# A mixture of experts on one core: experts in an order ranked by their tokens, four of them in rounds of 128 columns

## The reference

```python
g_idx = argmax(x @ router_g + b_g)                      # 1 of 4 groups
e_sel = (x @ router_e + b_e)[g_idx]                     # 8 logits in the group
top_v, top_i = top_k(e_sel, 2)
w = softmax(top_v) * softmax(g_logits)[g_idx]
out += w * (silu(x @ w1[e]) * (x @ w3[e])) @ w2[e]      # for both experts e
```

```
13 14 23 10 28 28 11 21 | 35  8 40 40 43 27 29 20 | 76 47 37 45 42 74 100 29 | 20 17 20 23 36 24 36 24
```

## Time and profile before

| | before |
|---|---|
| runs, us | 788.22, 794.74, 794.53; median 794.53 |
| profiled execution, us | 788.86 |
| its span, us | 787.1 |
| mean granted TensorE clock | 0.926 |
| PE / DVE / ACT / POOL busy | 84% / 38% / 26% / 10% |
| DMA | 189.86 MB, mean 241 GB/s |

### The profile page before, as it was taken

One profiled execution on the slowest core, in us unless ns is written; L12 is line 12 of the kernel. 1 busy time (PEld: TensorE's weight loads), 2 busy tenths in 40 slices (PEclk: granted clock), 3 DMA queues, 4 the chain that ended last, 5 costly groups with the idle time before them and its releaser, 6 DMA issues.

```text
span 787.1 us, 11931 instructions
## 1 busy us (share of the span) xinstructions
PE 660.6 (84%) x4993; PEld 470.0 (60%) x4993; DVE 300.1 (38%) x605; ACT 208.4 (26%) x359; POOL 80.8 (10%) x93
## 2 busy tenths in 40 slices
PE   4999997998999989999899549988878788889730
PEld 3999995678999989957787433333323233333210
DVE  3645575348533455785131821211111111111128
ACT  4613223044543334451031411211111111111113
POOL 0000002300002201000021111121111111111100
PEclk8899999999999999999899859999999889999965
DMA  9741312122755334899901955999999999979544
GB/s 284 227 132 55 108 54 80 33 73 68 201 134 195 108 101 132 286 300 307 381 22 68 409 191 226 420 419 420 421 419 420 420 420 420 414 287 417 244 167 165
DMA packets 76653, 189.86 MB, mean 241 GB/s; under 512 B 9878, under 2 KB 56658, under 8 KB 61736
## 3 DMA queue, kind: packets, MB, share of 16 engines
q1 hardware_dynamic: 63020, 145.09, 49.9%
q10 hardware_dynamic: 7404, 31.26, 9.7%
q0 software_dynamic: 6176, 12.76, 4.4%
HBM read 184.30 MB, written 16.66 MB: 255 GB/s over the span
## 4 chain that ended last, share of the span: by engine, by line
PE 59%; DMA 26%; DVE 7%; issue 3%; ACT 2%; SPq 1%; ACTq 1%; POOL 0%; POOLq 0%; DVEq 0%
DMA w<-exp_w 21%; PE ps L1844 11%; PE ps L1480 11%; PE ps L1482 11%; PE ps L1481 11%; PE ps L1586 4%; PE ps L1476 3%; PE ps L1871 2%; PE ps L1667 2%; DMA raw<-cache_mem_k 2%; DMA xe<-x_rows,gids 1%; DMA xs_rows<-x_sample 1%; PE ps L1604 1%; PE ps L1729 1%; DVE rstd L918 1%
## 5 line engine op out<-in xcount | busy, mean ns | idle before, releaser
L1844 PE MATMUL ps<-w,xeT 128*64 128x512 f32 x576 | 147.0, 669 | 31.2 <-DMA w<-exp_w 29.9
L1480 PE MATMUL ps<-xH,w_h 128*128 128x260 f32 x512 | 149.6, 292 | 11.7 <-DVE xL L944 5.2
L1482 PE MATMUL ps<-xL,w_h 128*128 128x260 f32 x512 | 146.5, 286 | 0.0
L1481 PE MATMUL ps<-xH,w_l 128*128 128x260 f32 x512 | 146.5, 286 | 0.0
L1844 PEld LDWEIGHTS ps<-w,xeT 128*64 128x64 f32 x576 | 50.8, 152 | 126.1 <-issue 121.5
L1480 PEld LDWEIGHTS ps<-xH,w_h 128*128 128x128 f32 x512 | 98.6, 193 | 17.2 <-DVE w_l L905 7.7
L1481 PEld LDWEIGHTS ps<-xH,w_l 128*128 128x128 f32 x512 | 98.4, 192 | 0.2
L1482 PEld LDWEIGHTS ps<-xL,w_h 128*128 128x128 f32 x512 | 98.4, 192 | 0.0
L905 DVE TENSOR_TENSOR w_l<-raw,w_h 128x2048 fp32r<-128x2048 f32 x28 | 64.1, 2289 | 35.3 <-ACT w_h L599 35.2
L1871 PE MATMUL ps<-w,aT 128*64 128x512 f32 x288 | 67.5, 611 | 11.1 <-DVE aT L1395 11.1
L1388 DVE SCALAR_TENSOR_TENSOR gated<-ps,rs_slot,silu 128x256 f32<-128x256 f32 x16 | 7.7, 484 | 158.3 <-ACT silu L841 158.3
(11 more groups left out here) (297 smaller groups left out, 884.6 us busy)
## 6 DMA issues: line engine op xcount, KB each, us to landing
w<-exp_w SPq DMA_DIRECT2D x81, 1024.0 KB, 19.1
w<-exp_w ACTq DMA_DIRECT2D x27, 1024.0 KB, 11.1
raw<-w_in SPq DMA_DIRECT2D x8, 1024.0 KB, 6.6
raw<-cache_mem_k SPq DMA_DIRECT2D x8, 1024.0 KB, 6.7
raw<-cache_mem_v SPq DMA_DIRECT2D x8, 1024.0 KB, 12.2
raw<-xa_wk SPq DMA_DIRECT2D x4, 1024.0 KB, 5.8
raw<-xa_wv SPq DMA_DIRECT2D x4, 1024.0 KB, 5.7
raw<-xa_wq SPq DMA_DIRECT2D x4, 1024.0 KB, 5.1
```

What stands on the lines that cost most here:

```text
L1480: pe.matmul(out, h1, h2, start=start, stop=False)
L1481: pe.matmul(out, l1, h2, start=False, stop=False)
L1482: return pe.matmul(out, h1, l2, start=False, stop=stop)
L1844: last = pe.matmul(mm[0][half, j, :], xeT[j][:, k, half], w13[s][:, :, k, :], start=k == 0, stop=k == KT_D - 1)
```

## The change

- Routing: PE counts the tokens of each expert twice, as a row on all partitions and as a column of 32 partitions (`count_ready`). DVE makes a key from count and number, compares all with all (`less`, `more_than`), and PE sums `less` to a rank. Experts 0 to 3, loaded already, get keys below all others. The four largest of the others get places 4, 9, 14 and 19 (`HEAVY`), the rest follow in falling order. Tables by place (`order`) and by rank (`blocks`) come out of one-hot matmuls, and the start of each expert's further items from a triangular matmul in place of five shifted additions on DVE.
- Rounds: places 4, 9, 14 and 19 are a round each, of 128 columns (`cap`), the others go in pairs: 16 rounds (still `PAIRS`) hold 28 places. Places 28 to 31 are the first four items of the loop, and items of over-full experts follow from the second pass on. `loops` is 1 when there are none.
- Loads: SP reads the expert's number from `order` in registers (`expert_at`) and issues all three matrices, w2 after a wait on `y_done`; ACT issues none. Expert 4's load became that of place 4 and waits for `order_ready`; `row_hot` lies elsewhere.
- `who`, `e_all` and the products are made by single operations for both choices and all tiles. `r2` sums `sumsq` and the last square, `zt[1]`, on PE, so that POOL adds seven blocks. POOL makes the constant rows by iota ahead, and PE turns two of them (`con`) between `so` and the second half of `wo`.

```diff
 CAP = P // 2
-PAIRS = EXPERTS // 2
-MORE_ITEMS = 2 * T // CAP
+SINGLES = 4
+ROUNDS = [(0, 1), (2, 3)]
+for _ in range(SINGLES):
+    p = ROUNDS[-1][-1] + 1
+    ROUNDS += [(p,), (p + 1, p + 2), (p + 3, p + 4)]
+ROUNDS += [(p, p + 1) for p in range(24, 28, 2)]
+PAIRS = len(ROUNDS)
+FIXED = 28
+OVER = 2 * T // CAP
+MORE_ITEMS = EXPERTS - FIXED + OVER
 COLS = PAIRS + MORE_ITEMS // 2 + 2
-KEY = 2048
 RING = 5
+ALL_ROUNDS = ROUNDS + [(28, 29), (30, 31)]
+BLOCK = [2 * q + n for q, r in enumerate(ALL_ROUNDS) for n in range(len(r))]
+HEAVY = [r[0] for r in ROUNDS if len(r) == 1]
+BY_RANK = HEAVY + [p for p in range(4, EXPERTS) if p not in HEAVY] + list(range(4))
+OVER_BLOCK = 2 * len(ALL_ROUNDS)
...
+            + ["ss", "sp", "or00", "or01", "or10", "or11", "so", "con", "r2", "lg", "pos", "list"])
...
-        row_hot = at("row_hot", [P, 2, NT, P], F32, e_at[4])
+        row_hot = at("row_hot", [P, 2, NT, P], F32, v_at)
...
-            sp.wait_ge(tv_ready, len(TV_ORDER))
-            load_gate_up(4, 4)
-            load_down(4, 4)
-            for q in range(2, PAIRS):
-                for e in (2 * q, 2 * q + 1):
-                    if e >= RING:
-                        sp.wait_ge(hid_ready, (e - RING) // 2 + 1)
-                        load_gate_up(e % RING, e)
+            sp.wait_ge(order_ready, 1)
+
+            def expert_at(p):
+
+                return sp.value_load(order[0:1, bass.ds(p, 1)], min_val=0, max_val=EXPERTS - 1)
+
+            e = expert_at(4)
+            load_gate_up(4, e)
+            load_down(4, e)
+            for q, places in enumerate(ROUNDS):
+                coming = [p + RING for p in places if p + RING < FIXED]
+                if coming:
+                    which = [expert_at(p) for p in coming]
+                    sp.wait_ge(hid_ready, q + 1)
+                    for p, e in zip(coming, which):
+                        load_gate_up(p % RING, e)
+                    sp.wait_ge(y_done, q + 1)
+                    for p, e in zip(coming, which):
+                        load_down(p % RING, e)
...
+                for r, slots in enumerate(((3, 4), (0, 1))):
+                    which = [expert_at(it * 4 + (FIXED + 2 * r + n)) for n in range(2)]
...
-                for e in (2 * q + RING, 2 * q + RING + 1):
-                    if e < EXPERTS:
-                        act.dma_start(w2s[e % RING][:].rearrange("p k d -> p (k d)"), w2[e]).then_inc(w2_in[e % RING], 16)
...
+            src = take("con")
+            dve.tensor_copy(con[:], src[0:EXPERTS, 0:2]).then_inc(tv_used, 1)
+            dve.tensor_tensor(through_of[:], upper[0:EXPERTS, 0:EXPERTS], ident[0:EXPERTS, 0:EXPERTS], ALU.add)
...
-            for j in range(NT):
-                last = dve.tensor_tensor(e_all[:, j], e_log[:, j], sel4[:, j], ALU.mult)
-            link(last)
+            link(dve.tensor_tensor(e_all[:], e_log, sel4, ALU.mult))
...
+                one = e_one[:, i].rearrange("p t (o e) -> p t o e", o=1).broadcast_to([P, NT, NG, NE])
+                link(dve.tensor_tensor(who[:, i].rearrange("p t (g e) -> p t g e", g=NG), one, sel4, ALU.mult))
+            dve.tensor_tensor(both[:], who[:, 0], who[:, 1], ALU.add).then_inc(who_ready, 1)
...
+            dve.wait_ge(route_made, 4)
+            dve.wait_ge(count_ready, 1)
+            counts = mm[0][:, 0, 0:EXPERTS]
+            dve.tensor_copy(count_p[:], mm[0][0:EXPERTS, 0, EXPERTS:EXPERTS + 1])
+            dve.scalar_tensor_tensor(key_p[:], mm[0][0:EXPERTS, 0, EXPERTS:EXPERTS + 1], float(EXPERTS), con[:, 0:1], ALU.mult, ALU.add)
+            link(dve.scalar_tensor_tensor(key_f[:], counts[0:EXPERTS], float(EXPERTS), key_row[0:EXPERTS], ALU.mult, ALU.add))
+            dve.tensor_scalar(less[:], key_f[:], key_p[:, 0:1], None, ALU.is_lt).then_inc(less_ready, 1)
+            link(dve.tensor_scalar(more_than[:], key_f[:], key_p[:, 0:1], None, ALU.is_gt))
+            link(dve.tensor_reduce(rank_p[:], more_than[:], AX_X, ALU.add))
+            link(dve.tensor_scalar(caps_p[:], rank_p[:], float(SINGLES), 1.0, ALU.is_lt, ALU.add))
+            dve.wait_ge(rank_ready, 1)
+            ranks = mm[0][:, 1, 0:EXPERTS]
+            dve.tensor_scalar(at_rank[:], ranks[0:EXPERTS], part_no[0:EXPERTS, 0:1], None, ALU.is_equal).then_inc(at_rank_ready, 1)
+            dve.tensor_scalar(caps[:], ranks, float(SINGLES), 1.0, ALU.is_lt, ALU.add)
+            link(dve.scalar_tensor_tensor(rank_f[:], caps_p[:], -float(CAP), count_p[:], ALU.mult, ALU.add))
+            link(dve.tensor_scalar(over_i[:, 0:1], rank_f[:], float(CAP - 1), 0.0, ALU.add, ALU.max))
+            link(dve.tensor_scalar(over_i[:, 1:2], over_i[:, 0:1], 6, None, ALU.arith_shift_right))
+            dve.tensor_copy(over_f[:], over_i[:, 1:2]).then_inc(over_ready, 1)
+            dve.tensor_scalar(at_place[:], rank_row[0:EXPERTS], rank_p[:, 0:1], None, ALU.is_equal).then_inc(at_place_ready, 1)
+
...
+            src = take("pos")[:, 0:NT * EXPERTS].rearrange("p (t e) -> p t e", t=NT)
+            dve.scalar_tensor_tensor(ptmp[:], each(caps[:]).broadcast_to([P, NT, EXPERTS]), -float(CAP), src,
+                                     ALU.mult, ALU.add).then_inc(tv_used, 1)
...
+            over_two = ptmp[:].rearrange("p (o t) e -> p o t e", o=1).broadcast_to([P, 2, NT, EXPERTS])
+            link(dve.tensor_tensor(wtmp[:], who[:], over_two, ALU.mult))
+            dve.tensor_reduce(place[:, 0], wtmp[:], AX_X, ALU.add)
+            dve.wait_ge(block_ready, 1)
+            link(dve.tensor_tensor(blocks[:], mm[1][:, 0, 0:EXPERTS], caps[:], ALU.add))
+            link(dve.tensor_scalar(blocks[:], blocks[:], 1.0 - CAP, float(CAP * OVER_BLOCK), ALU.mult, ALU.add))
+            dve.wait_ge(starts_ready, 1)
+            link(dve.scalar_tensor_tensor(packed[:], mm[1][:, 1, 0:EXPERTS], float(CAP), blocks[:], ALU.mult, ALU.add))
+            packed_b = each(packed[:]).broadcast_to([P, 2 * NT, EXPERTS])
+            flat = "p i t e -> p (i t) e"
+            link(dve.tensor_tensor(wtmp[:].rearrange(flat), who[:].rearrange(flat), packed_b, ALU.mult))
+            link(dve.tensor_reduce(place[:, 1], wtmp[:], AX_X, ALU.add))
+            link(dve.tensor_copy(place_i[:], place[:, 1]))
...
+            dve.tensor_scalar(bits[:, 0], place_i[:], CAP - 1, None, ALU.bitwise_and)
+            link(dve.tensor_scalar(bits[:, 1], place_i[:], 6, None, ALU.arith_shift_right))
+            link(dve.scalar_tensor_tensor(bits[:, 2], place[:, 0], 0.0, bits[:, 1], ALU.is_ge, ALU.mult))
+            link(dve.tensor_tensor(bits[:, 3], bits[:, 2], bits[:, 0], ALU.add))
+            link(dve.scalar_tensor_tensor(bits[:, 4], bits[:, 3], float(CAP), place[:, 0], ALU.mult, ALU.add))
+            dve.tensor_scalar(slot_i[:, 0], bits[:, 4], P - 1, None, ALU.bitwise_and)
+            link(dve.tensor_scalar(slot_i[:, 1], bits[:, 4], 7, None, ALU.arith_shift_right))
+            link(dve.tensor_copy(slot_f[:], slot_i[:]))
...
+            dve.wait_ge(place_ready, 1)
+            dve.tensor_copy(order[0:1, 0:EXPERTS], mm[0][0:1, 1, EXPERTS:2 * EXPERTS]).then_inc(order_ready, 1)
+            link(dve.tensor_copy(through[:], mm[1][:, 1, EXPERTS:2 * EXPERTS]))
...
-            dve.tensor_scalar(more_of[0:1], ends_n[0:1], float(EXPERTS - 1), None, ALU.min)
+            dve.tensor_scalar(order[0:1, EXPERTS:EXPERTS + OVER], ends_n[0:1], float(EXPERTS - 1), None, ALU.min)
...
+            link(dve.tensor_scalar(loops[0:1], total, 0.0, 1.0, ALU.is_gt, ALU.add))
+            for i in range(1, OVER // 4):
...
+            pe.wait_ge(route_made, 2)
+            out = open_tv("con")
+            pe.matmul(out[0:EXPERTS, 0:1], key_row[0:1, :], ones[0:1, 0:1], start=True, stop=True)
+            pe.matmul(out[0:EXPERTS, 1:2], block_row[0:1, :], ones[0:1, 0:1], start=True, stop=True).then_inc(tv_ready, 1)
...
-            pe.wait_ge(sq_added, 16)
             out = open_tv("r2")
+            pe.wait_ge(sq_added, 15)
+            pe.wait_ge(sq_ready, 16)
             for j, (t0, n) in enumerate(TILES):
-                last = pe.matmul(out[0:n, j:j + 1], sumsq[:, t0:t0 + n], ones[:, 0:1], start=True, stop=True)
+                for i, of in enumerate((sumsq, zt[1])):
+                    last = pe.matmul(out[0:n, j:j + 1], of[:, t0:t0 + n], ones[:, 0:1], start=i == 0, stop=i == 1)
...
+            pe.wait_ge(mm_used, len(MM_ORDER))
+            for j, (_, n) in enumerate(TILES):
+                pe.matmul(mm[0][:, 0, 0:EXPERTS], ones[0:n, :], both[0:n, j, :], start=j == 0, stop=j == NT - 1)
+            for j, (_, n) in enumerate(TILES):
+                last = pe.matmul(mm[0][0:EXPERTS, 0, EXPERTS:EXPERTS + 1], both[0:n, j, :], ones[0:n, 0:1],
+                                 start=j == 0, stop=j == NT - 1)
+            last.then_inc(count_ready, 1)
             out = open_tv("pos")
-            pe.matmul(out[:, 0:(NT + 1) * EXPERTS], upper[:], both[:].rearrange("p t e -> p (t e)"), start=True, stop=False)
...
```

(89 more changed lines are left out.)

92 lines of the change are left out of this document (54 added, 38 removed).

## The result

| | before | after |
|---|---|---|
| median of four runs, us | 794.57 (788.22 to 794.74) | 759.40 (756.11 to 761.22) |
| profiled execution / its span, us | 788.86 / 787.1 | 761.22 / 759.5 |
| mean granted TensorE clock | 0.926 | 0.937 |

The ratio is 0.9581, with a 95% interval of 0.9546 to 0.9617, which is 33 us less; the two medians of the table lie 35.2 us apart. The changed kernel was run again beside later experiments and gave 757.13 against 791.58, a ratio of 0.9568 (0.9542 to 0.9593).

The account below looks back on a forecast made before the run. The rounds were taken as bound by the DMA bytes of the weights. Terms -30.1 - 3 + 3.1 + 0.5 - 1.0 = -30.5 us gave 758.4 from the profiled execution and 764.1 from the median; forecast the middle, 761, range 751 to 774.

Parts of the forecast that it names:

- Bytes, 36 experts to 32, 30.1 us: Weight loads of the rounds: four experts fewer, 12.6 MB at 418 GB/s, 30.1 us saved.
- which limit holds: Rounds: DMA lets the last `hidden` begin near 702, PE at 689, so DMA stays the limit by some 13 us.
- Rounds of one expert cost as much as pairs: Rounds on PE: one expert takes 7.2 and 3.6 us against a pair's 7.04 and 3.65; period 12.7, bounds 12.7 to 13.1.
- PE at full clock to round 13, first wait at round 14: Rounds on PE: granted clock 1.00 without weight waits through round 13, then a first wait of 5 to 10 us.
- The hole at the loop, -3: DMA dip where the loop begins, 307 of 418 GB/s: larger backlog fills it, gain 0 to 5.8 us, taken as 3.
- Routing, +3.1: Routing chain on PE and DVE before the rounds: `slot_f` done 3.1 us later, bounds 2 and 6.
- First gather, -1.0: Start of the rounds: less of place 4's load left beside the gather, landing 1.0 us sooner.
- One queue, nothing: Weight loads all on SP's queue: waits for `y_done` make nothing late, issue lies beside `hidden`, cost nothing.
- A: Rival: weights fully continuous, routing free; 36.4 us saved, 752 against the profiled execution; chance 0.07 (below 752).
- C: Rival: gathers in the rounds land late, over 1% slower from landings of 20.2 us; 810 at 21 us; chance 0.04.
- D: Rival: token counts force a second loop pass, 36 experts loaded in 20 rounds; 789 to 798 us; chance 0.06.
- B: Rival: PE becomes the rounds' limit, period 13.5 us in place of 12.7; 765 to 773 us; chance 0.15.

## Why the prediction was right

The forecast was 761 us, with a range of 751 to 774, and the measured 759.4 lies in it. The mechanism is the one described: the bytes of four experts, saved in a stage bound by the DMA. That 759.4 lies as near as 1.6 us to 761 is in part luck. The sum of -30.5 gives 764.1 from the median of the runs, and the 761 is halfway from there to the 758.4 that it gives from one fast execution; the medians themselves moved by 33 to 35 us. Point by point:

- **Bytes, 36 experts to 32, 30.1 us.** Measured 96 loads, one pass, 92.6 MB in the stretch, and 30.4 to 30.5 us less from first to last `hidden`. The size is right. The reason given ahead of it, 12.6 MB at 418 GB/s, was not enough by itself: without loads in the loop the kernel before gains 4 us. What made the bytes count is that light rounds lie between heavy ones, so that DMA and PE both stay full. The prediction's part on which limit holds had this, but as a check and not as a condition.
- **Rounds of one expert cost as much as pairs.** 7.13 + 3.70 against 7.04 + 3.65; period 12.8 to 12.9. Inside the bounds. The page "TensorEngine Tiling (Array Packing)" of the Trainium skill, section "Theoretical Speedup", gives up to a factor of two at 64 or less, and the trace agrees: 32 instructions at 64 columns, for two experts, take what 16 at 128 take for one.
- **PE at full clock to round 13, first wait at round 14.** The first wait was 0.86 us at round 10, the first large one at round 13, one round early, with 3.5 us where 5 to 10 had been reckoned. The granted clock is 1.00 up to 605, as forecast.
- **The hole at the loop, -3.** This step failed. The DMA still fell to 359 and 377 GB/s, and the run that filled the slot a round earlier moved the dip without a gain. The larger backlog that was to fill the queue there was gone by 657. The term should have been 0: from the first to the last `hidden` 30.4 to 30.5 us were gained, which is the bytes' 30.1 and no more.
- **Routing, +3.1.** From the last residual addition to `gids` it is 27.9 and 27.7 us against 26.6, so +1.1 to +1.3. Three parts make the 1.9 us between forecast and measurement. The largest is the counts' 20 small instructions at 0.138 each: the ten with one column took 0.56 us together, and all twenty 1.8 in place of 2.8. PE began them 11.4 us after that addition, where `pos` had begun after 11.9, so the shorter `who` was worth 0.5 and not nothing. And the part from the counts to `slot_f` was 7.2 us long in place of 7.6.
- **`con`, +0.5.** The `wo` matmuls start 0.3 us later.
- **First gather, -1.0.** It landed in 6.5 us in place of 8.2. From the last addition to the first `hidden` 38.9 and 38.4 us stand against 39.3 and 39.2, so routing and gather together are -0.3 to -0.9 where +2.1 had been reckoned. The gather's term by itself, from `gids` to the first `hidden`, is 11.0 and 10.7 us in place of 12.7 and 12.6: -1.7 to -1.9, which is nearly twice the -1.0.
- **One queue, nothing.** Two experiments gave 0 to 2 us. SP's waits cost nothing, though its issues stretched (below).
- **The sum** came to -30.5, of which -33.1 for the rounds. Measured by stages it is -30.4 for the rounds and -0.3 to -0.9 for the way to them. So the sum owes its size to errors of opposite sign: 2.7 too much for the rounds, and 2.4 to 3.0 too little for routing and gather. The end, from the last `hidden` on, had been put at 48 us as before; it is 48.2 and 50.0 in the profiles of before and 47.8 and 46.0 in those of the changed kernel. There PE's clock is sometimes low after the last wait (7.09 + 3.65 us for `hidden` and `down` in one execution of the changed kernel, 8.78 + 5.35 in one of before). Two profiles of each can't tell how much of the 0.4 to 4 us is the change and how much is scatter.
- **Rivals.** A (continuous weights, free routing) had the routing nearly right and the DMA wrong. C (late gathers) fell: none landed later than 11.0 us. The page "DMA: Bandwidth & Descriptors" of the Trainium skill, section "Queues, rings and completion order", says that each engine goes round its queues packet by packet, and the 13.7 that became 10.1 with one queue less agree with it. D (a second pass) didn't occur. B's period of 13.5 didn't either, but its remark that two near limits both cause waits did come true: the rounds lose 11.7 us to waits, and without any they would still need 226.7, so that further bytes saved could bring, as an estimate, about 12 us and what the low clock behind the waits costs.

## What to carry to other kernels

When loads are the limit of a stage, saving bytes helps only in steps where the compute can follow faster; make the ratio of bytes to compute as even as the buffers reach, and put the light steps between the heavy ones. Before filling a dip in the bandwidth, ask who waits for the bytes. At the start of such a stage, let the small transfer that starts the compute go ahead of a large load that is needed only later.
